# Dilated attention: scaling the exponentials while they are turned, in place of scaling y

## The reference, cut to what matters

```python
def dilated_group_attention(q, k, v, win, dil, bias_table):
    ...
    s = jnp.einsum('brnqhe,brnkhe->brnhqk', qs, kk) + bias
    s = jnp.where(mask[None, None, :, None], s, -jnp.inf)
    m = jnp.max(s, axis=-1, keepdims=True)
    p = jnp.exp(s - m)
    l = jnp.sum(p, axis=-1, keepdims=True)
    ...
    o = jnp.einsum('brnhqk,brnkhe->brnqhe', p, vv) / lt

def dilated_attention_mixer(qkv, rel_bias):
    ...
    w = l_all * jnp.exp(m_all - jnp.max(m_all, axis=0, keepdims=True))
    o = jnp.sum(w * o_all, axis=0) / jnp.sum(w, axis=0)
```

## Time and profile before

| | us |
|---|---|
| median of 3 runs | 1343.15 |
| lowest, highest | 1340.04, 1345.56 |
| profiled execution | 1342.11 |
| its span | 1340.2 |
| TensorE busy in the span | 1324.5 |
| VectorE busy | 870.3 |
| ScalarE busy | 721.7 |
| the attention, first turned block to the end of the last values | 32.0 |

### The profile page before, as it was taken

One profiled execution on the slowest core, in us unless ns is written; L12 is line 12 of the kernel. 1 busy time (PEld: TensorE's weight loads), 2 busy tenths in 40 slices (PEclk: granted clock), 3 DMA queues, 4 the chain that ended last, 5 costly groups with the idle time before them and its releaser, 6 DMA issues.

```text
span 1340.2 us, 22440 instructions
## 1 busy us (share of the span) xinstructions
PE 1324.5 (99%) x8876; PEld 1197.7 (89%) x8876; DVE 870.3 (65%) x1140; ACT 721.7 (54%) x1070; POOL 49.9 (4%) x76
## 2 busy tenths in 40 slices
PE   8999999999999999999999999999999999999999
PEld 7998899999899779999999899889999888899997
DVE  6889888885898566555565675565555577655554
ACT  3666644444644556444466763555555666655553
POOL 0100000000111000000001000000000000000000
PEclk8999999999899999999999999999999999999999
DMA  9978789985699624555537444455555552355540
GB/s 353 388 267 278 268 282 316 311 297 185 234 358 353 198 59 146 188 186 187 188 140 232 155 140 144 129 169 191 188 190 188 171 168 95 126 189 189 188 156 32
DMA packets 147362, 275.54 MB, mean 206 GB/s; under 512 B 4728, under 2 KB 85392, under 8 KB 147161
## 3 DMA queue, kind: packets, MB, share of 16 engines
q1 hardware_dynamic: 132176, 220.21, 48.7%
q0 software_dynamic: 13872, 52.05, 11.5%
q10 hardware_dynamic: 1240, 2.26, 0.5%
HBM read 273.40 MB, written 1.10 MB: 205 GB/s over the span
## 4 chain that ended last, share of the span: by engine, by line
PE 86%; DVE 6%; DMA 4%; issue 2%; ACT 2%; SPq 0%; ACTq 0%; DVEq 0%
PE ps L1985 84%; DMA raw<-in_ada_w 2%; DMA ada_ring<-in_ada_w 2%; DVE acc_a L1223 2%; DVE wlo L1210 1%; PE ps L2126 1%; PE ps L2362 1%; DMA raw<-in_hyb_w_in 1%; ACT whi L513 0%; ACT xn L567 0%; DVE xn L1324 0%; PE ps L2470 0%; ACT small L574 0%; DVE x L1318 0%; PE ps L2663 0%
## 5 line engine op out<-in xcount | busy, mean ns | idle before, releaser
L1210 DVE TENSOR_TENSOR wlo<-raw,whi 128x1024 fp32r<-128x1024 f32 x400 | 485.5, 1224 | 356.0 <-ACT whi L513 354.5
L513 ACT CAST whi<-raw 128x1024 fp32r<-128x1024 f32 x400 | 417.6, 1051 | 472.8 <-PE ps L1985 456.7
L1985 PE MATMUL ps<-hhi,whi 128*128 128x256 f32 x1792 | 507.4, 283 | 2.9 <-DVE hlo L1371 2.4
L1985 PE MATMUL ps<-hhi,wlo 128*128 128x256 f32 x1792 | 500.7, 279 | 0.0
L1985 PE MATMUL ps<-hlo,whi 128*128 128x256 f32 x1792 | 499.9, 279 | 0.0
L1985 PEld LDWEIGHTS ps<-hhi,whi 128*128 128x128 f32 x1792 | 335.9, 187 | 9.1 <-issue 6.2
L1985 PEld LDWEIGHTS ps<-hlo,whi 128*128 128x128 f32 x1792 | 336.2, 188 | 4.7 <-issue 2.4
L1985 PEld LDWEIGHTS ps<-hhi,wlo 128*128 128x128 f32 x1792 | 336.5, 188 | 0.0
L1985 PE MATMUL ps<-whi,hidhi 128*128 128x512 f32 x432 | 170.3, 394 | 0.0
L1985 PE MATMUL ps<-wlo,hidhi 128*128 128x512 f32 x432 | 169.1, 392 | 0.0
L1985 PE MATMUL ps<-whi,hidlo 128*128 128x512 f32 x432 | 168.6, 390 | 0.0
(11 more groups left out here) (238 smaller groups left out, 1156.6 us busy)
## 6 DMA issues: line engine op xcount, KB each, us to landing
raw<-in_ffn_w_in SPq DMA_DIRECT2D x44, 1024.0 KB, 6.4
ada_ring<-in_ada_w POOLq DMA_DIRECT2D x40, 1024.0 KB, 7.3
raw<-in_w_mlp_up SPq DMA_DIRECT2D x32, 1024.0 KB, 5.4
raw<-in_w_mlp_down SPq DMA_DIRECT2D x32, 1024.0 KB, 5.0
raw<-in_ffn_w_out SPq DMA_DIRECT2D x22, 1024.0 KB, 5.0
raw<-in_att_w_qkv SPq DMA_DIRECT2D x18, 1024.0 KB, 6.8
raw<-in_w_in_even SPq DMA_DIRECT2D x18, 1024.0 KB, 4.9
raw<-in_hyb_w_in SPq DMA_DIRECT2D x10, 1024.0 KB, 12.0
```

Source lines behind the costliest of these rows:

```text
L513: A.copy(whi[:, H % 4, :], raw[:, slot(n), h * HALF:(h + 1) * HALF]).then_inc(s["hi_ready"], 1)
L1210: V.tensor_tensor(wlo[:, H % 4, :], raw[:, slot(n), h * HALF:(h + 1) * HALF], whi[:, H % 4, :].bitcast(F32), ALU.subtract).then_inc(s["lo_ ...
L1985: return pe.matmul(out, lhsT, rhs, start=first, stop=last, skip_group_check=True)
```

## The change

The exponentials are no longer transposed but multiplied by a diagonal matrix: block^T times diag(1/sum). This turns a block and scales each of its queries. So the values come out as the finished y; the rows of reciprocals and the multiplication of y are left out, and `dl_hi` and `dl_lo` read y from bank 2 of PSUM.

- VectorE makes the diagonals: `dl_shares(p, hd)` takes a head's two reciprocals and multiplies the identity by each, into four of eight blocks of `ada_ring` behind the 18 of `pt2`. For the first head of pair 0 this stands between two splits, for the first head of a later pair between the two biased scores of the pair's second head, for each second head behind the copy of unit 1.
- TensorE's units 0 and 1 wait for the first head's diagonals, units 2 to 4 for the second's. A unit's matmuls are plain float32 products.
- The fifth unit is two blocks wide, and its copy 256 columns.
- ScalarE makes both exponentials of the next pair's first head ahead of the copy of unit 4; before, one stood behind it.
- The values of a pair wait for the remainder of the last y (`dl_ylo`), before for its multiplication (`dl_y`).
- At the end `gate_gain(3)` no longer stands behind a wait for the last values.

```diff
-        pt2, yd = ada_flat[:, 0:20 * P], ada_flat[:, 20 * P:20 * P + S]
+        pt2 = ada_flat[:, 0:18 * P]
+        def dl_diag(p, hd, tt):
+            a = 18 + 4 * (p % 2) + 2 * hd + 1 - tt
+            return ada_flat[:, a * P:(a + 1) * P]
...
-            return 4 * i, 4 * i + 4
+            return 4 * i, min(4 * i + 4, 18)
...
             def dl_hi(p):
-                act.wait_ge(s["dl_y"], p + 1)
-                A.copy(hhi[:, p, :], yd).then_inc(s["dl_yhi"], 1)
+                act.wait_ge(s["dl_o"], p + 1)
+                A.copy(hhi[:, p, :], ps[:, 2, 0:S]).then_inc(s["dl_yhi"], 1)
...
                 if p < 3:
                     dl_exp(p + 1, 0, 1)
+                    dl_exp(p + 1, 0, 0)
                 dl_copy(p, 4)
-                if p < 3:
-                    dl_exp(p + 1, 0, 0)
...
+                    if shares and tt == 0:
+                        dl_shares(p, 0)
                     V.tensor_tensor_reduce(out=out.rearrange("p (g s) -> p g s", g=DG), in0=src, in1=win,
...
-            def dl_rcp(p):
-                dve.wait_ge(s["dl_e"], 4 * p + 4)
-                V.reciprocal(small[:, 2, 4 * p:4 * p + 4], small[:, 1, 4 * p:4 * p + 4]).then_inc(s["dl_r"], 1)
-            def dl_norm(p):
-                dve.wait_ge(s["dl_o"], p + 1)
-                V.tensor_tensor(yd, ps[:, 2, 0:S], pt2[:, 18 * P:20 * P], ALU.mult).then_inc(s["dl_y"], 1)
+            def dl_shares(p, hd):
+                k = 4 * p + 2 * hd
+                dve.wait_ge(s["dl_e"], k + 2)
+                link(V.reciprocal(small[:, 2, k:k + 2], small[:, 1, k:k + 2]))
+                V.tensor_scalar(dl_diag(p, hd, 1), ident[:, :], small[:, 2, k:k + 1], None, ALU.mult)
+                V.tensor_scalar(dl_diag(p, hd, 0), ident[:, :], small[:, 2, k + 1:k + 2], None, ALU.mult) \
+                    .then_inc(s["dl_r"], 1)
...
             split(HV + 6)
+            dl_shares(0, 0)
             split(HV + 7)
             for p in range(4):
-                if p:
-                    dl_norm(p - 1)
                 dl_copy(p, 1)
-                dl_rcp(p)
+                dl_shares(p, 1)
                 if p:
                     dl_lo(p - 1)
                 if p < 3:
                     dl_scores(p + 1, 0)
                 dl_copy(p, 3)
                 if p < 3:
-                    dl_scores(p + 1, 1)
-            dl_norm(3)
+                    dl_scores(p + 1, 1, True)
             gate_gain(3)
             dl_lo(3)
...
             def dl_turn(p, i):
-                pe.wait_ge(s["dl_e"], 4 * p + (2 if i < 2 else 4))
+                pe.wait_ge(s["dl_r"], 2 * p + (1 if i < 2 else 2))
...
-                if i == 4:
-                    dl_rows(p)
-                for j in range(j0, min(j1, 18)):
-                    m = pe.transpose(dl_turned(p, i)[:, (j - j0) * P:(j - j0 + 1) * P], dl_block(p, j), ident[:, :])
+                for j in range(j0, j1):
+                    m = mm(dl_turned(p, i)[:, (j - j0) * P:(j - j0 + 1) * P], dl_block(p, j),
+                           dl_diag(p, j // 9, 1 if j % 3 else 0))
...
                         if p:
-                            pe.wait_ge(s["dl_y"], p)
+                            pe.wait_ge(s["dl_ylo"], p)
```

More of the change, by code:

```diff
@@ L79 @@
 vec_dil vec_dil_c vec_out vec_swa
-bias_in0 bias_in1 bias_in2 dl_bias0 dl_bias1 dl_s0 dl_s dl_z dl_e dl_t dl_tc dl_td dl_o dl_r dl_y dl_yhi dl_ylo gate_added
+bias_in0 bias_in1 bias_in2 dl_bias0 dl_bias1 dl_s0 dl_s dl_z dl_e dl_t dl_tc dl_td dl_o dl_r dl_yhi dl_ylo gate_added
 even_in nr_sq nr_ssq nr_ln nr_r nr_done rp_rot rp_done
@@ L830, in dl_copy @@
                 act.wait_ge(s["dl_t"], 5 * p + i + 1)
-                A.copy(pt2[:, j0 * P:j1 * P], dl_turned(p, i)).then_inc(s["dl_tc"], 1)
+                A.copy(pt2[:, j0 * P:j1 * P], dl_turned(p, i)[:, 0:(j1 - j0) * P]).then_inc(s["dl_tc"], 1)
             def dl_hi(p):
-                act.wait_ge(s["dl_y"], p + 1)
-                A.copy(hhi[:, p, :], yd).then_inc(s["dl_yhi"], 1)
+                act.wait_ge(s["dl_o"], p + 1)
+                A.copy(hhi[:, p, :], ps[:, 2, 0:S]).then_inc(s["dl_yhi"], 1)
             HV = 2 * FIRST["qkv"] + 32
@@ L1570, in _, with dl_scores @@
                     ada_block(acc_a, 14 + b, 512 * b)
-            def dl_scores(p, hd):
+            def dl_scores(p, hd, shares=False):
                 h = 2 * p + hd
@@ L1592, in dl_copy @@
                 V.tensor_copy(pt2[:, j0 * P:j1 * P], dl_turned(p, i)).then_inc(s["dl_td"], 1)
-            def dl_rcp(p):
-                dve.wait_ge(s["dl_e"], 4 * p + 4)
-                V.reciprocal(small[:, 2, 4 * p:4 * p + 4], small[:, 1, 4 * p:4 * p + 4]).then_inc(s["dl_r"], 1)
-            def dl_norm(p):
-                dve.wait_ge(s["dl_o"], p + 1)
-                V.tensor_tensor(yd, ps[:, 2, 0:S], pt2[:, 18 * P:20 * P], ALU.mult).then_inc(s["dl_y"], 1)
+            def dl_shares(p, hd):
[5 more added lines that the diff above has]
+                    .then_inc(s["dl_r"], 1)
             def dl_lo(p):
                 dve.wait_ge(s["dl_yhi"], p + 1)
-                V.tensor_tensor(hlo[:, p, :], yd, hhi[:, p, :].bitcast(F32), ALU.subtract).then_inc(s["dl_ylo"], 1)
+                V.tensor_tensor(hlo[:, p, :], ps[:, 2, 0:S], hhi[:, p, :].bitcast(F32), ALU.subtract).then_inc(s["dl_ylo"], 1)
             HV = 2 * FIRST["qkv"] + 32
```

## The result

| | before | after |
|---|---|---|
| median of 11 runs, us | 1344.03 | 1349.51 |
| lowest, highest | 1340.03, 1345.75 | 1346.28, 1351.24 |
| profiled execution | 1342.11 | 1349.14 |
| its span | 1340.2 | 1347.3 |
| the stage (first turned block to the end of the last values) | 31.99 | 37.65 |

The kernel after is slower: ratio 1.0045, 95% interval 1.0034 to 1.0056, or +6.0 us (4.6 to 7.5). The forecast was 1347.0, +3.8. The median after is 2.5 us over it and lies in the forecast's range, 1340.7 to 1352.0; +6.0 lies within the 0.5% (6.7 us) called no change, though the interval reaches over that. The mechanism was as forecast, but the cost of turning a block was sized too small: the stage is 5.66 us longer, and the sum's own bounds ended at +5.3. The time is in the range because that had 2 us of scatter on top.

What follows compares the result with a forecast made beforehand. TensorE, busy 99% of the span, was taken to bound the kernel. Terms +6.23, -2.36, -1.74, +1.53 and +0.1 summed to +3.8 us, giving 1347.0 us against the median 1343.15, with range 1340.7 to 1352.0.

Steps and rivals of the forecast that it cites:

- TensorE bounds the stage, and its time goes through to the end: Attention stage: TensorE, busy 99% of the span with 86% of the chain, passes any added or removed time on.
- Products: TensorE: 72 transposes at 0.1275 us become float32 products at 0.214 us, adding 6.23 us.
- Rows of reciprocals, -2.36: TensorE: eight recorded instructions, 0.59 us in each of four pairs, are removed, saving 2.36 us.
- Waits for copies, -1.74: TensorE's transposes: waits for a copy to free a PSUM bank vanish under longer units, saving 1.74 us.
- The hole, +1.53: First pair, between units 1 and 2: TensorE waits for VectorE's second-head diagonals, adding 1.53 us.
- Waits of the next pair, +0.1: First head of later pairs: new waits of hundredths, 0.1 us for three pairs together.
- Rival C: Chain of copy, exponentials and diagonals becomes the bound: +3.0 us more, in all +6.8, 1350; chance 0.14.
- Rival A: TensorE's 72 products show weight loads fully, 0.38 us each: +12 us on top, 1359; chance 0.04.
- rival B: TensorE: a product costs four transposes, 0.51 us: +21.3 us more, 1368.3; chance 0.02.
- D: TensorE: a product is one record at 0.1275 us, no dearer than a transpose: -2.4 us, 1340.7; chance 0.06.

Runs made afterwards that it cites:

- the experiment that keeps them: Kernel before with its 72 transposes replaced by float32 products with the identity; stage 38.92 us, +6.93.
- the exchanged order: Kernel after with ScalarE's earlier order, one exponential of the next pair's first head behind the copy of unit 4; stage 37.65 us, the same.
- the rounded products: Kernel after with the first pair's second-head diagonals made early, exponentials and diagonals held as float32r; stage 30.41 us, ratio 0.9997 against the kernel before.

## Why the prediction came out as it did

- *TensorE bounds the stage, and its time goes through to the end*: right. The stage is 5.66 us longer, the span behind it is not shorter (848.5 and 848.3 us).
- *Products*: the step that was mis-sized. I took 0.1275 for a transpose (1.02 us divided by eight) and 0.214 for a product (1.71 divided by eight). Both are whole groups from start to start, and what lies at the ends of a group isn't proportional to it. Eight records 0.109 apart are 0.87, so the 1.02 holds 0.15 us that belongs to its ends; sixteen 0.112 apart are 1.79, so the 1.71 is cut short by the matmul of another shape behind it. The kernel before had a row that shows this, which I read past; here it is with the same place in the kernel after. Ahead of matmuls of 512 columns both groups are 0.17 us shorter than ahead of the scores:

```profile
480.80 1.09 PE L2362 MATMUL ps<-ident,prob 128*128 128x128 f32 x8
```
```profile
486.94 2.05 PE L1989 MATMUL ps<-ada_ring,prob 128*128 128x128 f32 x16
488.75 0.48 PE L1989 MATMUL ps<-whi,hhi 128*128 128x512 f32 x1
```

Eight transposes take 0.85 us there (to 481.65) and 1.02 before the scores, eight products 1.81 and 1.98. I had divided the long form of the one and the short form of the other. Like against like it is 0.96 us for eight in both places, 0.12 a block with the ends of the group in it. By differences of groups a block is 0.108 or 0.109 and 0.223: the term is 72 x 0.114 = 8.2 us, not 6.2. The bounds that I gave the product (0.20 to 0.224) held; the transpose had none, and that is where most of the error was (0.0185 us a block of 0.0275).
- *Rows of reciprocals, -2.36*: right; none are left, and the experiment that keeps them shows the same 0.59 us each.
- *Waits for copies, -1.74*: nearly. The named ones are gone, but about 0.1 us a pair stays before unit 4. The forecast compared the unit with the copy alone (0.59); the copy's whole way is 0.18 + 0.59 + 0.12 = 0.89 us, as long as a unit of 0.89, so this cover is just at its end.
- *The hole, +1.53*: right in place and cause; without it the first pair is 1.53 us shorter and the stage 1.49.
- *Waits of the next pair, +0.1*: none is seen, and no score waits for its bias, as forecast. Rival C, which would have made them large, fell with the exchanged order.
- The sum by the measured terms is 8.2 - 2.36 - 1.74 + 0.44 + 1.49 = 6.0 us. The stage has 5.66. The other 0.4 us lie at the ends of groups, which the sum leaves out. Unit 4's two transposes were a group of their own between the rows and the values, 0.37 us (463.09 to 463.46) where two of 0.109 are 0.22; with the rows these ends went too, 0.15 a pair, 0.6 in all. Against them a group of products before the scores has 1.98 - 1.79 = 0.19 us at its ends where a group of transposes had 0.15, by an estimate 0.2 us over the stage.
- *Rival A* (unhidden weight loads) would have been 0.38 a product, *rival B* 0.51, *D* 0.1275: none was it. D's one record a product came true for the rounded products only. The 4 times of the Trainium skill's page "TensorE: Matmul & The Clock Gate", section Terms, is 2 in this kernel, 0.223 against 0.109, for blocks of 128 x 128 by 128 columns. The advice of its page "Perfetto Trace Analysis", section Transposes, held for float32 products; the rounded ones were as cheap as transposes.

## What to carry to other kernels

In these runs a product with a diagonal cost no more than a transposition when it was one record (float32r); in float32 it was two, and those 0.114 us a block were more than the rows and waits saved. Take the price of one instruction from the difference of two groups of different count, not from a group's length divided by its count, compare groups that stand before the same kind of work, and bound the price of what is removed as well. Where the pacing engine's work is made shorter, the waits that it had covered come back: of the 8 us that the one-pass products saved, 5.75 reached the stage. A transfer that waits for its buffer is one of those waits: the bias's 5 us were hidden at 8.8 us a pair and showed in the kernels with shorter units.

## What the runs showed that I had not expected

- The start of the stage scatters by more than the whole change: in ten profiles it starts between 457.59 and 467.33 us. Its length was the same to 0.01 us in two kernels that differ only in ScalarE's order (37.65 twice, and 30.41 twice).
- For 128 x 128 by 128 columns a float32 transpose and a float32r product are one record, 0.11 us from the next, and a float32 product is two, each 0.11 from the next.
- A multiplication of 128 columns on VectorE lasts 0.28 us, against 0.35 for 256: 0.2 us from start to start.
